# Stick-breaking stage: other slots for the out-projection's products, gating and residual sums

## What is computed

```python
def stick_breaking(q, k, v, q_pos, k_pos):
    z = jnp.einsum('bqhd,bkhd->bhqk', q, k).astype(jnp.float32) * (HEAD_DIM ** -0.5)
    mask = k_pos[None, :] < q_pos[:, None]
    log_keep = jnp.where(mask, jax.nn.log_sigmoid(-z), 0.0)
    after = lax.cumsum(log_keep, axis=3, reverse=True) - log_keep
    w = jnp.where(mask, jnp.exp(jax.nn.log_sigmoid(z) + after), 0.0)
    return jnp.einsum('bhqk,bkhd->bqhd', w.astype(v.dtype), v)

def combine(x, sb_o, sb_gate, win_o, win_gate, w_out):
    mixed = jnp.concatenate([sb_o * jax.nn.silu(sb_gate), win_o * jax.nn.silu(win_gate)], axis=-1)
    return x + mixed @ w_out
```

## The kernel before

| | q=1 | q=2 | q=3 |
|---|---|---|---|
| sigmoid, silu_gate, gate_o | 3, 5, 7 | 4, 7, 9 | 4, 7, 9 |
| split_hi, split_lo | 8, 9 | 10, 11 | 10, 11 |
| tiles of half 0 | 4 a slot, 11 and 12 | 2 a slot, 13 to 16 | 1 a slot, 15 to 22 |
| residual of half 0 | 13 | 17 | 23 |
| tiles of half 1 | 4 a slot, 14 and 15 | 2 a slot, 19 to 22 | 1 a slot, 24 to 31 |
| residual of half 1 | 15 | 23 | 31 |

## Time and profile before

### The profile page before, as it was taken

The page is one execution under the profiler, slowest core; times in us unless marked ns, Lnnn a source line. Parts: engine busy times, 40 slices in busy tenths (PEclk is TensorE's granted clock), DMA queues, the critical chain, the costliest instruction groups (busy, mean ns, idle before and its releaser), DMA issues. The chain is left out here.

```text
span 1842.6 us, 26108 instructions
## 1 busy us (share of the span) xinstructions
PE 1540.9 (84%) x7514; PEld 1248.0 (68%) x7514; DVE 1116.9 (61%) x1405; ACT 873.2 (47%) x1864; POOL 571.2 (31%) x460
## 2 busy tenths in 40 slices
PE   4699979998999999899946577887788878888768
PEld 4577758786877788687835556666666656666557
DVE  5355515333433543343337777779998999998932
ACT  7322224333533443343316655556676666676621
POOL 1101011110210110110107834435555455454442
PEclk8899989998998999899967789889999989899889
DMA  4011134413422342243125343335334233233033
GB/s 186 29 52 52 63 110 129 122 58 111 137 68 80 104 127 80 71 139 100 63 68 187 112 137 108 109 102 156 94 113 127 78 109 106 71 105 97 3 92 117
DMA packets 181391, 183.08 MB, mean 99 GB/s; under 512 B 18448, under 2 KB 128904, under 8 KB 181304
## 3 DMA queue, kind: packets, MB, share of 16 engines
q1 hardware_dynamic: 181304, 181.92, 32.4%
HBM read 118.13 MB, written 63.93 MB: 99 GB/s over the span
## 5 line engine op out<-in xcount | busy, mean ns | idle before, releaser
L1216 POOL TENSOR_TENSOR c_weight<-c_take,c_kept 128x512 f32<-128x512 f32 (+2 forms) x320 | 351.7, 1112 | 325.8 <-DVE c_kept L1334 225.6
L255 PE MATMUL b_ps<-XH,w_w_hi 128*128 128x512 f32 (+1 forms) x800 | 303.5, 379 | 15.2 <-issue 8.3
L1334 DVE TENSOR_TENSOR_SCAN c_kept<-c_keep,c_kept 128x513 f32<-128x513 f32 x192 | 311.6, 1623 | 2.5 <-ACT c_keep L1260 1.4
L256 PE MATMUL b_ps<-XL,w_w_hi 128*128 128x512 f32 (+1 forms) x800 | 302.6, 378 | 0.0
L257 PE MATMUL b_ps<-XH,w_w_lo 128*128 128x512 f32 (+1 forms) x800 | 301.4, 377 | 0.0
L1394 PE MATMUL c_score<-c_k,c_q_hi 128*128 128x512 f32 (+2 forms) x320 | 154.8, 484 | 122.9 <-ACT c_take L1264 111.5
L1272 ACT ACTIVATE c_w_hi<-c_turn 128x512 fp32r<-128x512 f32 (+1 forms) x320 | 173.4, 542 | 117.6 <-PE c_turn L1406 116.9
L1340 DVE TENSOR_TENSOR c_w_lo<-c_turn,c_w_hi 128x512 fp32r<-128x512 f32 (+1 forms) x320 | 187.9, 587 | 56.9 <-ACT c_w_hi L1272 55.7
L1260 ACT ACTIVATE c_keep<-c_score 128x512 f32<-128x512 f32 (+2 forms) x320 | 171.6, 536 | 103.3 <-DVE c_kept L1334 97.7
L248 POOL TENSOR_TENSOR w_w_lo<-w_w_raw,w_w_hi 128x1024 fp32r<-128x1024 f32 x27 | 64.8, 2400 | 481.5 <-ACT w_w_hi L243 481.5
L666 ACT ACTIVATE b_raw<-b_ps 128x512 f32<-128x512 f32 x80 | 47.8, 597 | 304.0 <-PE b_ps L257 299.2
(11 more groups left out here) (230 smaller groups left out, 2831.8 us busy)
## 6 DMA issues: line engine op xcount, KB each, us to landing
c_k<-k_parts SPq DMA_DIRECT2D x80, 256.0 KB, 3.5
c_v<-v_parts SPq DMA_DIRECT2D x80, 256.0 KB, 4.5
w_w_raw<-in_w_in SPq DMA_DIRECT2D x27, 512.0 KB, 4.3
x_rows<-in_x_prompt SPq DMA_DIRECT2D x4, 2048.0 KB, 10.2
b_qraw<-normT SPq DMA_DIRECT2D x32, 256.0 KB, 4.1
k_parts<-b_kpart SPq DMA_DIRECT2D x16, 512.0 KB, 2.9
v_parts<-b_vpart SPq DMA_DIRECT2D x16, 512.0 KB, 3.2
gateT<-b_raw SPq DMA_DIRECT2D x32, 256.0 KB, 2.0
```

The source lines that it names most:

```text
L255: pe.matmul(out, w.hi[n][:, dt, :], xh, start=(dt == 0), stop=False)
L256: pe.matmul(out, w.hi[n][:, dt, :], xl, start=False, stop=False)
L1216: pool.tensor_tensor(weight[:, st.par, j, 0:n], take[:, j, 0:n], kept[:, j, 1:n + 1], ALU.mult).then_inc(weighted, 1)
L1334: dve.tensor_tensor_scan(kept[:, j, down], keep[:, j % 2, down], keep[:, j % 2, down], above, ALU.mult, ALU.bypass).then_inc(scanned, 1)
```

## The change

Only the slots are changed. No instruction, tile, wait or buffer is added or taken away. `TILES` becomes a list of the slot of each tile, `RESIDUAL` gives the slots of the two residual sums, and five tables give the slots of the gating; q = 1 has its own, q = 2 and 3 share one.

```diff
-        TILES = {1: (4, 11, 14), 2: (2, 13, 19), 3: (1, 15, 24)}
+        TILES = {1: ([7, 7, 8, 8, 9, 9, 10, 10], [11, 12, 12, 13, 13, 13, 14, 14]),
+                 2: ([8, 9, 10, 11, 12, 13, 14, 15], [16, 17, 18, 19, 20, 21, 21, 22]),
+                 3: ([8, 9, 10, 11, 13, 14, 15, 16], [18, 19, 21, 22, 23, 25, 26, 28])}
+        RESIDUAL = {1: (11, 15), 2: (16, 23), 3: (18, 30)}
+        SIGMOID, SILU, GATE_O, SPLIT_HI, SPLIT_LO = (
+            {q: at if q > 1 else first for q in range(1, NSB)}
+            for first, at in ((0, 0), (2, 3), (4, 5), (5, 6), (6, 7)))
...
-                        if q and (u, n) == ((1, 1) if q == 1 else (1, 3)):
+                        if q and 4 * u + n == SILU[q]:
                             proj.silu_gate(dve, r)
-                        if q and (u, n) == ((1, 3) if q == 1 else (2, 1)):
+                        if q and 4 * u + n == GATE_O[q]:
                             proj.gate_o(dve, r)
-                        if q and (u, n) == ((2, 1) if q == 1 else (2, 3)):
+                        if q and 4 * u + n == SPLIT_LO[q]:
                             proj.split_lo(dve, r)
```

More of the change, by code:

```diff
@@ L1090, in projection_tiles @@
                 return []
-            each = TILES[q][0]
-            return [(half, n) for half in range(2) for n in range(DT)
-                    if n // each == 4 * u + s - TILES[q][1 + half]]
+            return [(half, n) for half in range(2) for n in range(DT) if TILES[q][half][n] == 4 * u + s]
         def residual_due(q, u, s):
[L1097 to L1101, removed]
+            return [half for half in range(2) if q and RESIDUAL[q][half] == 4 * u + s]
         def iterations(eng, body):
@@ L1282, in body @@
                     due = q_due(q, p, u, last)
[L1283 to L1308, removed]
+                    for n in range(QB):
+                        if n == 3 and not q:
+                            proj.split_w_hi(act, 2 * p + u, u, p)
+                        if n == 3 and u and Step(q, p, u - 1).last:
+                            finish(Step(q, p, u - 1))
+                        back_hi(st, u, n)
+                        if nxt:
+                            sigmoids(nxt, n)
+                        if n == 0 and due:
+                            q_hi_part(due, due.q + 1 if due.e else q + 1)
+                        if q and 4 * u + n == SIGMOID[q]:
+                            proj.sigmoid(act, 4 * (q - 1) + p)
+                        if q and 4 * u + n == SPLIT_HI[q]:
+                            proj.split_hi(act, 4 * (q - 1) + p)
                 finish(st)
```

## The result

The changed kernel takes 1870.12 us (median of 4 runs, 1868.27 to 1870.52) against 1847.27 us of the kernel before on the same chip: a ratio of 1.012, 95% interval 1.0091 to 1.015. It is 1.2% slower. The forecast was 1861 us, slower by 0.6%; the range of 1829 to 1884 us holds the result, the chance given to "slower by over 1%" was 0.28.

What follows compares the result with a forecast made beforehand. DVE was taken to bound q=2 and q=3, and DVE then PE to set q=1's pace. Terms of -0.5 (q=1), +8.0 (q=2) and +4.4 us (q=3) gave +11.9 on 1848.9, so 1861 us; range 1829 to 1884.

Steps and rivals of the forecast that it cites:

- PE's waits: PE stands some 5 to 6 us at slot 8 for split_lo, and waits for residual sums in slots 11, 16, 18.
- ACT's wait for the gate at the start of q=1: At p=0 of q=1, ACT's gate wait grows from 3.42 to about 7.5 us; charged +1.5.
- iteration lengths named as signs: Signs of being right: iterations of 44 to 45 us at q=1, 57 to 59 at q=2, 76 to 77 at q=3.
- q=1: DVE's part 5.2 us shorter, PE's 4.8 longer, smaller terms; -0.5 an iteration, +1.5 at p=0, sum -0.5 us.
- q=3: Slot 8 +1.1, slots 18 and 19 +0.9, the end -0.9 us an iteration; +4.4 us over four.
- neighbouring waits at 18 and 19: At q=3, PE idles some 3.6 us at 18; DVE loses 3.2 us in place of 2.3: +0.9 an iteration.
- The wait in slot 8: At q=3, low clock after it; DVE loses 2.0 to 2.2 us, POOL gives some back: +1.1 an iteration.
- q=2: Slot 8 +0.5 us and the residual in slot 16 +1.5 us an iteration; +8.0 us over four.
- slot 16: +1.5: At q=2, PE's residual wait before short diagonal scans: +0.5 at the high clock or +2.6 at the low; middle taken.
- Rival A: The clock holds at the waits in slots 7/8, 11/16/18; sum -18 us, 1831 us; chance 0.25.
- Rival B: Low clock at every wait, no return from POOL; sum +34 us, 1883 us; chance 0.27.
- Rival C: Nothing moves: DVE's own work stays the same, waits only change names; within 4 us, 1849 us; chance 0.13.

Runs made afterwards that it cites:

- half 1 back: Changed kernel with only the tiles of half 1 of q=2 at their old slots 19 to 22: 1857.19 us, 1.0067 of the kernel before.
- only the gating early: Changed kernel with only the gating steps in their new slots, all tiles and residual sums in their old ones: 1858.8 us, 1.0073 of before.
- the same, extra matmuls in slot 15: The kernel with only the gating steps moved, plus 14 extra matmuls in slot 15 of q=2: 1852.03 us, 1.0031 of the kernel before.
- extra matmuls in slot 16: Changed kernel with 8 extra matmuls in slot 16 of q=2, ahead of the residual-sum wait: 1865.16 us, 1.0111 of before; profiled run 1858.31 us.
- old order, extra matmuls: Kernel before, all places old, with extra matmuls in PE's own waits at q=1, 2 and 3: 1836.91 us, 0.9948 of the kernel before.
- first filler run: Changed kernel with extra matmuls before PE's waits in slots 7, 11 (q=1), 8, 16 (q=2), 8, 18 (q=3): 1842.16 us, 0.9973 of before.
- mixed kernel: Changed kernel with q=2 as in the kernel before, and extra matmuls in PE's waits of all three blocks: 1829.64 us, 0.9915 of before.

## Why the prediction was right or wrong

The direction and the mechanism (PE's lead is lost at the new waits, and the low clock behind them makes DVE wait) were right. The size fell short of the measured one, 0.6% against 1.2%, and the step that was too small is q=2. That q=1 and q=3 came out near their sums is partly luck, as told below.

**PE's waits.** Predicted at slot 8: 5 to 6 us of idle time, released by `p_m_lo`. Measured: 5.38, 4.25 and 6.54 us at p=1 of q=1, 2 and 3, and new waits for `p_y` in slots 11, 16 and 18 of 1.77, 2.02 and 2.50 us. ACT's wait for the gate at the start of q=1 was put at 7.5 us and is 7.66 (ACT's L957 after). Of the iteration lengths named as signs, q=2 lies outside its 57 to 59 us (59.8 to 61.6), q=1 to both sides of its 44 to 45 (43.3 or 45.3), and q=3 at its 76 to 77 (76.2 to 77.5) but for the last iteration (70.7).

**q=1**, predicted -0.5 in sum, measured -0.8. The terms were of the right kind: at p=1 PE's part starts 6.9 us earlier and is 5.3 us longer. But the same old places took 181.5 us in another kernel, so a difference of under 4 us isn't told here, and the agreement is luck in part. One iteration, p=2, is 45.3 us long in place of 43.3 or 43.4. Most of that (1.5 of 2.0 us) lies behind slot 11: its wait is 1.77 us in every iteration, yet the clock stayed at 1.00 behind it at p=1 and was 0.50 at p=2. Kernel after, behind slot 11 at p=1, then at p=2:

```profile
1145.00:1150.00 5.00, 5.00 (x27) 4.22 (x28) 3.01 (x3) 2.65 (x6) 2.01 (x2) 1.00 0.53 157
1189.20:1192.20 3.00, 3.00 (x11) 2.41 (x10) 0.63 (x1) 0.35 (x1) 1.09 (x1) 0.50 0.78 221
```

**q=3**, predicted +4.4, measured +4.7. The sum came out, the split does not, and that is luck: the last iteration is 1.2 us shorter and the other three 1.1 to 2.4 longer, and the same places took 297.4 to 301.9 us in four kernels. The neighbouring waits at 18 and 19 took less than I charged (2.50 us at PE, not 3.6), DVE lost 1.04 and 0.89 us there in place of 1.6 and 1.6. The wait in slot 8 took more (DVE's waits in slots 9 to 11: 1.50, 1.34 and 0.50 us against 0.5, 1.5 and 0.2).

**q=2**, predicted +8.0, measured +17.4: the failed term. DVE's finish in slot 15 cuts each iteration in two, and the two terms of the prediction (slot 8: +0.5 an iteration; slot 16: +1.5) lie on either side of it. Sums over the four iterations, us:

| kernel | up to the finish in slot 15 | from there to the last finish |
|---|---|---|
| before | 142.5 | 83.1 |
| after | 150.8 | 92.2 |
| half 1 back | 150.8 | 78.6 |
| only the gating early | 145.3 | 90.0 |
| the same, extra matmuls in slot 15 | 145.2 | 82.5 |
| extra matmuls in slot 16 | 148.5 | 85.8 |
| old order, extra matmuls | 142.4 | 82.5 |

*Up to slot 15* the prediction had +2.0 in all, and +8.3 were measured: this is the larger part of the miss. DVE's idle time there went from 2.1 to 8.7 us and its busy time from 140.4 to 142.1. For slot 8 I had counted 1.3 us of lost time an iteration, of which 0.8 would come back through POOL. But the early gating alone, costed at nothing, makes this part 2.8 us longer (145.3), and the extra matmuls behind it don't change that (145.2). The other 5.5 us come with the tiles at slot 8 and after; no run held the clock throughout this part, so how much of them is clock stays open.

*From slot 15 on* the prediction had +6.0 in all, and +9.1 were measured. From the release in slot 16 to the end of the iteration it gave 17.9 us at the high clock and 20.0 at the low one, and took the middle. The two values were good: 19.6 us at p=1 of the kernel after, where the clock was 0.51, and 18.0 in the kernel with extra matmuls in slot 16, where it was 1.00. The choice of the middle failed; the case was the low clock. I had bounded it with single waits from other blocks and not asked how many stand close together: 2.02 us of idle time followed 1.75 in the slot before.

This also reads the 13.6 us of the run with half 1 back: its first part is that of the changed kernel (150.8), its second one is 4.5 us shorter than before, so the new places of half 1 cost 9.1 us against the old order and 13.6 against that run.

The gating was taken as work of a fixed length that could stand anywhere. Alone, with all tiles in their old slots, it costs 9.6 us at q=2: 2.8 up to slot 15, the rest behind it, and the held clock gives back 7.5. That part is a wait that was there all along and was covered: PE's first mix of a new head waits for DVE's finish in slot 15. Before, PE came late to it; with the gating early PE is early, stands idle, and loses its clock ahead of the narrow slots. The changed kernel comes to slot 15 with less lead (1.75 us of idle time in place of 3.4). The costs of the parts don't add up, because each decides how far ahead PE is when it meets the next wait.

The 2.8 us are DVE's own busy time: with the clock held in both, DVE is busy 144.9 of the 145.2 us up to slot 15 with the gating early, and 142.1 of 142.4 in the old order. In the kernel before, a full-width scan that follows gate_o takes 1.28 us, in the same order of work without the gating ahead of it 1.75: POOL's product has run while DVE was at the gating. The first of these rows is of the kernel before, the other two, a scan and the product beside it, of the run with the gating early:

```profile
1323.44 1.28 DVE L1334 TENSOR_TENSOR_SCAN c_kept<-c_keep,c_kept 128x513 f32<-128x513 f32 x1
```

```profile
1324.38 1.75 DVE L1325 TENSOR_TENSOR_SCAN c_kept<-c_keep,c_kept 128x513 f32<-128x513 f32 x1
1323.96 1.09 POOL L1219 TENSOR_TENSOR c_weight<-c_take,c_kept 128x512 f32<-128x512 f32 x1 [2.30 <-DVE c_kept L1325]
```

Early gating at q=2 stands between the narrow diagonal scans, where there is less to give back. That it is this that makes up the 2.8 us was read from the rows, not tried by itself. The Trainium skill (SBUF — State Buffer, Who interferes with whom) says that a DVE instruction with two inputs in SBUF contends with a GpSimd instruction that reads SBUF; the scan reads two such inputs, and by that the trace agrees: 1.75 us with a product running into it, 1.28 without. The same section of the Trainium skill has an exclusive lock, by which the scan would stand until the product ends. In the rows the product ends at 1325.05, 0.67 us after the scan starts, and the scan is 0.47 us longer. So most of the overlap is lost; POOL's spans are rough, and no run here settles whether all of it is.

**Rival A** (the clock holds, 1831 us) did not happen in the changed kernel, but its sum can be compared with the runs with extra matmuls: q=1 was put at -8.5 and is -10.7 (174.5 against 185.2), q=3 at -11.6 and is -4.8 to -9.4 (292.4 in the first filler run, 287.8 in the mixed one). Its condition, a wait in slot 8 of under about 2 us, was not met: the waits there were 3.28 us and more. And the value is no safe bound: the clock fell behind waits of 2.02 and, in some iterations, 1.77 us. **Rival B** (the low clock at every wait, 1883 us) had its condition met more often than not: the clock was 0.51 behind slot 16 at q=2, 0.51 from 1.4 us after slot 18's wait at q=3 (1615.8 to 1619.3), and low behind slot 11 in two of four iterations of q=1. Its sum was near for q=2 (predicted +15.6, measured +17.4), its prices for q=3 (+12.4) and q=1 (+6) were too high. **Rival C** held that DVE's own work is the same in any order. At q=2 it is not: 53.6 us in place of 52.1.

## What to carry to other kernels

Where two engines pace each other, cost a reordering by the lead: at each wait ask how far ahead the faster engine comes to it, and what clock it has when it leaves. A step that is moved forward makes its user early, and an early user stops at the next wait, perhaps one that was covered until now. If low-clock stretches behind short waits are on the path, matmuls on constant data into a free bank can hold the clock, if they are sized to the wait at the high clock and start before it falls; here that brought the old order to 0.9948 of before and the mixed kernel to 0.9915, where the new order of the work alone gave 1.012. And before a block of a trace is compared with another, see how far it repeats where nothing was changed.

## What the runs showed of the hardware

PE's granted clock was 0.51 for the next 3.5 us after an idle time of 2.02 us in slot 16, with 1.75 us of idle time in the slot before it; with eight matmuls in the second wait it stayed at 1.00 (1343.4 to 1350.0 us of that kernel). The same idle time did not always do the same: 1.77 us in slot 11 of q=1 was followed by a clock of 1.00 at p=1 and of 0.50 at p=2. At q=2 of the kernel with the first filler it fell after an idle time of 2.9 us for want of scores. After the clock was down, 12 matmuls of 512 columns took 5.34 us; the 14 in slot 15 of the run with the gating early, at the high clock, took 3.38.

A full-width scan took 1.28 us with no product of POOL beside it and 1.75 us with 0.67 us of one.

The start of the block q=1 in the profiled executions varies between 1059.7 and 1069.6 us with the same work ahead of it, almost half of the effect studied. How far a block's length repeats depends on the block: q=2 of the old order took 225.6, 225.5 and 225.5 us in three kernels, q=1 of the old order 185.2 and 181.5 in two, q=3 of the new order 297.4 to 301.9 in four. At q=2 a comparison by block was far sharper than the medians; at q=1 and q=3 it wasn't.
